# Query tiles of the routing stage start on rows that are not yet normed; root and shift are applied to their products

## The reference

```
def rms_norm(x, g, eps=RMS_EPS):
    y = x32 * lax.rsqrt(jnp.mean(x32 * x32, axis=-1, keepdims=True) + eps)
    return (y * g.astype(jnp.float32)).astype(x.dtype)
...
        mod = (jax.nn.silu(c) @ w_ada[l] + b_ada[l])[:, None, :]
        sh1, sc1, gt1, sh2, sc2, gt2 = jnp.split(mod, 6, axis=-1)
...
        h = h + gt1 * (mixed @ w_out[l])
        xn2 = rms_norm(h, norm2_g[l]) * (1.0 + sc2) + sh2
        h = h + gt2 * peer_ffn(xn2, peer_wq[l], peer_subkeys[l], peer_u[l], peer_v[l])
...
def peer_ffn(xn, wq, subkeys, u_tab, v_tab):
    q = (xt @ wq).reshape(T, PEER_HEADS, 2, PEER_HALF)
    s = jnp.einsum('thpd,hpnd->thpn', q, subkeys).astype(jnp.float32)
    top_s, top_i = lax.top_k(s, PEER_TOPK)
```

## Time and profile before

| | before |
|---|---|
| median of 3 runs | 1678.75 us (1678.7 to 1679.78) |
| profiled execution, its own time | 1680.06 us |
| its span | 1678.1 us |
| PE busy | 1636.5 us, 98% of the span |
| DVE busy | 1238.0 us, 74% |
| ACT busy | 821.5 us, 49% |
| mean granted TensorE clock | 0.998 of full speed |

### The profile page before, as it was taken

One profiled execution on the slowest core, in us unless ns is written; L12 is line 12 of the kernel. 1 busy time (PEld: TensorE's weight loads), 2 busy tenths in 40 slices (PEclk: granted clock), 3 DMA queues, 4 the chain that ended last, 5 costly groups with the idle time before them and its releaser, 6 DMA issues.

```text
span 1678.1 us, 32665 instructions
## 1 busy us (share of the span) xinstructions
PE 1636.5 (98%) x11608; PEld 1440.7 (86%) x11608; DVE 1238.0 (74%) x2593; ACT 821.5 (49%) x1491; POOL 165.5 (10%) x135
## 2 busy tenths in 40 slices
PE   6999999999999999999999999999999999999998
PEld 4887988899988888888888888888899777999998
DVE  6885537748989988788888888888446565578887
ACT  3544111345469944555555555555444246554443
POOL 0020000007700000000000000000037214100000
PEclk9999999999999999999999999999999999999999
DMA  8742135765742288777777777777454651245553
GB/s 345 289 145 89 40 126 209 269 202 172 220 151 63 89 261 261 233 238 237 237 236 234 237 233 238 237 236 233 142 175 132 221 183 39 90 137 186 178 186 126
DMA packets 102623, 316.94 MB, mean 189 GB/s; under 512 B 11393, under 2 KB 21377, under 8 KB 102145
## 3 DMA queue, kind: packets, MB, share of 16 engines
q1 hardware_dynamic: 101664, 311.27, 57.4%
q10 hardware_dynamic: 864, 4.39, 0.7%
HBM read 309.71 MB, written 5.90 MB: 188 GB/s over the span
## 4 chain that ended last, share of the span: by engine, by line
PE 68%; DVE 11%; ACT 9%; issue 8%; DMA 2%; DVEq 0%; POOL 0%; SPq 0%; ACTq 0%
PE bank L490 9%; PE bank L492 9%; PE bank L491 9%; PE bank L505 4%; PE bank L1949 4%; PE bank L1951 4%; PE bank L1953 4%; PE bank L1212 3%; ACT whi L479 3%; PE bank L506 2%; ACT arena L1912 2%; PE bank L465 2%; PE bank L1498 2%; ACT arena L1903 2%; DVE xn L2071 2%
## 5 line engine op out<-in xcount | busy, mean ns | idle before, releaser
L484 DVE TENSOR_TENSOR wlo<-wring,whi 128x1024 fp32r<-128x1024 f32 x340 | 414.2, 1223 | 88.9 <-ACT whi L479 80.0
L479 ACT CAST whi<-wring 128x1024 fp32r<-128x1024 f32 x386 | 403.7, 1046 | 115.7 <-PE bank L1953 49.5
L490 PE MATMUL bank<-xboth,whi 128*128 128x256 f32 x1184 | 340.3, 287 | 5.7 <-DVE wlo L484 2.6
L491 PE MATMUL bank<-xboth,whi 128*128 128x256 f32 x1184 | 334.9, 283 | 0.0
L492 PE MATMUL bank<-xboth,wlo 128*128 128x256 f32 x1184 | 334.9, 283 | 0.0
L490 PEld LDWEIGHTS bank<-xboth,whi 128*128 128x128 f32 x1184 | 226.9, 192 | 11.1 <-issue 5.6
L491 PEld LDWEIGHTS bank<-xboth,whi 128*128 128x128 f32 x1184 | 227.1, 192 | 0.7 <-issue 0.5
L492 PEld LDWEIGHTS bank<-xboth,wlo 128*128 128x128 f32 x1184 | 227.0, 192 | 0.0
L505 PE MATMUL bank<-xboth,whi 128*128 128x512 f32 x616 | 220.8, 397 | 0.0
L484 POOL TENSOR_TENSOR wlo<-wring,whi 128x1024 fp32r<-128x1024 f32 x46 | 117.6, 2561 | 855.2 <-ACT whi L479 855.0
L506 PE MATMUL bank<-xboth,wlo 128*128 128x256 f32 x616 | 172.7, 280 | 0.0
(11 more groups left out here) (384 smaller groups left out, 2730.2 us busy)
## 6 DMA issues: line engine op xcount, KB each, us to landing
wring<-in_w SPq DMA_DIRECT2D x463, 512.0 KB, 4.1
arena<-in_ada SPq DMA_DIRECT2D x48, 512.0 KB, 7.2
xn<-in_ada SPq DMA_DIRECT2D x96, 256.0 KB, 3.2
h_spill<-arena SPq DMA_DIRECT2D x37, 128.0 KB, 2.0
arena<-h_spill SPq DMA_DIRECT2D x37, 128.0 KB, 4.2
wring<-in_w SPq DMA_DIRECT2D x6, 384.0 KB, 4.8
wring<-in_w SPq DMA_DIRECT2D x8, 256.0 KB, 3.3
arena<-in_const ACTq DMA_DIRECT2D x1, 1215.0 KB, 5.5
```

Source lines behind the costliest of these rows:

```text
L479: act.copy(whi[:, n % HSLOTS, :], wring[:, n % SLOTS, :]).then_inc(hi_ready, 1)
L484: eng.tensor_tensor(wlo[:, n % SLOTS, :], wring[:, n % SLOTS, :], whi[:, n % HSLOTS, :].bitcast(F32), ALU.subtract).then_inc(lo_ready, 1)
L490: pe.matmul(out, h, xh, start=start, stop=False, **kw)
L491: pe.matmul(out, h, xl, start=False, stop=False, **kw)
```

## The change

The first nine of the sixteen query tiles (`RAW1` = 9) are computed on `raw`, a split copy of `hT` times the gain, without the root. Two more columns in each block of `raw` hold the shift, so that a matmul has 258 columns and column 256 of the bank holds the product of weights and shift. DVE multiplies the bank by the reciprocal root into `qp` and copies that column out (`raw_scale`), and ACT adds it (L1811 of the changed kernel). The normed rows, which the other seven tiles and later stages need, are made between these steps, block by block. The rows of `ada` for the scale are fetched first, so that the gain is known before w_out starts. The last two sums of squares move from w_out into the first pair of tiles, and the 22 matmuls on the identity are gone.

```
+        def raw_upper(act, n, m):
+            act.activation(raw[:, m, 0, 0:S], hT[:, m, :], ACT.Identity, scale=gsc[:, n, m:m + 1]).then_inc(x_hi, 1)
+        def raw_rest(dve, n, m):
+            dve.wait_ge(x_hi, XHI[n] + m + 1)
+            dve.scalar_tensor_tensor(raw[:, m, 1, 0:S], hT[:, m, :], gsc[:, n, m:m + 1], raw[:, m, 0, 0:S].bitcast(F32),
+                                     ALU.mult, ALU.subtract).then_inc(x_lo, 1)
+        def raw_pair(pe, norm, n, outs):
+            for k0, k1 in ((0, KT - 2), (KT - 2, KT)):
+                for i in range(2):
+                    pe.wait_ge(lo_ready, nth_split[n + i])
+                    for k in range(k0, k1):
+                        pe.wait_ge(x_lo, XLO[norm] + k + 1)
+                        mm = raw_three(pe, outs[i], n + i, k)
+                    if k1 == KT:
+                        mm.then_inc(tile_done, 1)
+                    elif i == 0:
+                        for m in range(k1, KT):
+                            norm_sum(pe, norm, m, nsq[norm])
+        def raw_scale(dve, out, bk, rt, add):
+            dve.tensor_tensor(out, bk[:, 0:S], rt, ALU.mult)
+            return dve.tensor_copy(add, bk[:, S:S + 1])
+        def norm_gain(dve, n, k, rt):
+            dve.scalar_tensor_tensor(xn[:, k, :], hT[:, k, :], gsc[:, n, k:k + 1], rt, ALU.mult,
+                                     ALU.mult).then_inc(x_scaled, 1)
+        def norm_upper(act, n, k, shift):
+            act.wait_ge(x_scaled, KT * n + k + 1)
+            act.activation(xhi[:, k, :], xn[:, k, :], ACT.Identity, bias=modc(shift, k)).then_inc(x_hi, 1)
+        def norm_rest(dve, n, k, shift):
+            dve.wait_ge(x_hi, XHI[n] + KT + k + 1)
+            dve.scalar_tensor_tensor(xlo[:, k, :], xn[:, k, :], modc(shift, k), xhi[:, k, :].bitcast(F32), ALU.add,
+                                     ALU.subtract).then_inc(x_lo, 1)
...
         def pe_w_out(pe):
...
-            for m in (KT - 2, KT - 1):
-                norm_sum(pe, 1, m, nsq[1])
-            pe_warm(pe, 7, 22)
...
         def act_w_out(act):
...
+                raw_upper(act, 1, m)
                 act_square(act, 1, m, nsq[1])
...
         def pe_route(pe):
...
+            raw_pair(pe, 1, w, (bank[r % BANKS], bank[(r + 1) % BANKS]))
+            for t in range(2, RAW1):
+                pe.wait_ge(lo_ready, nth_split[w + t])
+                pe.wait_ge(ring_free, r + t - BANKS + 1)
+                raw8(pe, bank[(r + t) % BANKS], w + t).then_inc(tile_done, 1)
+            pe.wait_ge(x_lo, XLO[2])
+            ring_tiles_split(pe, "wq", RAW1)
...
             for t in range(COUNT["wq"]):
                 act_hi_of(act, "wq", t + 2)
                 tile_wait(act, "wq", t)
-                act.copy(qp[:, t, :], ring_bank("wq", t)[:, 0:S]).then_inc(ring_free, 1)
+                if t < RAW1:
+                    act.wait_ge(raw_scaled, t + 1)
+                    act.activation(qp[:, t, :], qp[:, t, :], ACT.Identity, bias=raw_add1[:, t:t + 1]).then_inc(ring_free, 1)
+                    for k in (2 * t - 4, 2 * t - 3):
+                        if 0 <= k < KT:
+                            norm_upper(act, 1, k, 3)
...
             norm_root(dve, v, 1, rtn[1])
-            norm_scale(dve, rtn[1])
-            x_rest(dve, 1)
-            lo_phase(dve, "wq", 2)
+            lo(2)
+            norm_gain(dve, 1, 0, rtn[1])
+            norm_gain(dve, 1, 1, rtn[1])
+            scale(0)
+            scale(1)
+            lo(3)
+            for t in range(2, RAW1):
+                lo(t + 2)
+                for k in (2 * t - 2, 2 * t - 1):
+                    if k < KT:
+                        norm_gain(dve, 1, k, rtn[1])
+                    else:
+                        norm_rest(dve, 1, k - KT, 3)
+                scale(t)
+            for t in range(RAW1 + 2, COUNT["wq"]):
+                lo(t)
```

More of the change, by code:

```diff
@@ L167 @@
 ARENA = 41920
+RAW = S + 2
+RAW_AT = 18736
+RAWNORMS = (1, )
+XHI, XLO = [0], [0]
+for _name in range(4):
+    XHI.append(XHI[-1] + (2 * KT if _name in RAWNORMS else KT))
+    XLO.append(XLO[-1] + (2 * KT if _name in RAWNORMS else KT // 2))
 AFTER_WHI = S * NK + 2 * KT * S + HSLOTS * D
@@ L209, in build_layer_pair @@
         sb("xn_end", [P, AHALF])
-        sb("arena_start", [P, S * NK])
+        sb("arena_start", [P, RAW_AT])
+        raw = sb("raw", [P, KT, 2, RAW], F32R)
+        sb("arena_middle", [P, S * NK - RAW_AT - 2 * KT * RAW])
         xboth = sb("xboth", [P, KT, 2, S], F32R)
@@ L533, in act_square @@
             act.activation(sq[:, m, :], hT[:, m, :], ACT.Square).then_inc(sq_ready, 1)
-            if n in (1, 3) and m == KT - 3:
+            if n in (1, 3) and m == 1:
                 act_table(act, ACT.Sqrt)
@@ L595, in x_rest_pair @@
         def x_rest_pair(eng, n, k):
[L597 removed]
+            eng.wait_ge(x_hi, XHI[n] + k + 2)
             eng.tensor_tensor(xlo[:, k:k + 2, :], xn[:, k:k + 2, :], xboth[:, k:k + 2, 0, :].bitcast(F32),
@@ L609, in split_pair @@
                 if k % 2 == 0:
-                    pe.wait_ge(x_lo, 4 * norm + k // 2 + 1)
+                    pe.wait_ge(x_lo, XLO[norm] + k // 2 + 1)
                 for i in range(2):
@@ L618, in build_layer_pair, with raw_shift_upper, raw_shift_rest @@
         rtn = [arena[:, 5632:5888], arena[:, 28672:28928], r2["rot"][:, 0:256], rF["sg"][:, 0:256]]
+        raw_scaled = sem("raw_scaled")
+        def raw_shift_upper(act, shift):
+            act.copy(raw[:, :, 0, S:RAW], wide(modc(shift, 0, KT), 2))
+        def raw_upper(act, n, m):
+            act.activation(raw[:, m, 0, 0:S], hT[:, m, :], ACT.Identity, scale=gsc[:, n, m:m + 1]).then_inc(x_hi, 1)
+        def raw_shift_rest(dve, n, m, shift):
+            dve.wait_ge(x_hi, XHI[n] + m + 1)
+            dve.tensor_tensor(raw[:, :, 1, S:RAW], wide(modc(shift, 0, KT), 2), raw[:, :, 0, S:RAW].bitcast(F32), ALU.subtract)
@@ new lines, in raw_rest, with raw_three @@
+        def raw_rest(dve, n, m):
+            dve.wait_ge(x_hi, XHI[n] + m + 1)
+            dve.scalar_tensor_tensor(raw[:, m, 1, 0:S], hT[:, m, :], gsc[:, n, m:m + 1], raw[:, m, 0, 0:S].bitcast(F32),
+                                     ALU.mult, ALU.subtract).then_inc(x_lo, 1)
+        def raw_three(pe, out, n, k):
+            return three(pe, out[:, 0:RAW], n, k, raw[:, k, 0, :], raw[:, k, 1, :], k == 0, k == KT - 1)
+        def raw_pair(pe, norm, n, outs):
[10 more added lines that the diff above has]
+                            norm_sum(pe, norm, m, nsq[norm])
@@ new lines, in raw8 @@
+        def raw8(pe, out, n):
+            for k in range(KT):
+                mm = raw_three(pe, out, n, k)
+            return mm
+        def raw_scale(dve, out, bk, rt, add):
[4 more added lines that the diff above has]
+                                     ALU.mult).then_inc(x_scaled, 1)
@@ new lines, in norm_upper, with norm_whole @@
+        def norm_upper(act, n, k, shift):
[5 more added lines that the diff above has]
+                                     ALU.subtract).then_inc(x_lo, 1)
+        def norm_whole(act, n, k, shift):
+            act.wait_ge(x_lo, XLO[n] + KT + k + 1)
+            act.activation(xn[:, k, :], xn[:, k, :], ACT.Identity, bias=modc(shift, k)).then_inc(xn_ready, 1)
@@ L857, in ada @@
                     sp.wait_ge(ada_used, 3 * KT + i - BSLOTS + 1)
-                sp.dma_start(aringb[:, i % BSLOTS, :], a["ada"][3 * KT + i]).then_inc(blanded[i % BSLOTS], 16)
+                sp.dma_start(aringb[:, i % BSLOTS, :], a["ada"][late_row(i)]).then_inc(blanded[i % BSLOTS], 16)
             sp.wait_ge(t_new, 10)
@@ L1638, in dve_proj @@
                 dve_late_ada(dve, m)
+                if m == SCALE_AT:
+                    dve.wait_ge(ada_used, 4 * KT)
+                    dve_add_bias(dve, v, 4 * KT, 5 * KT)
+                    dve_gsc(dve, v, 1)
+        SCALE_AT = next(j for j in range(KT) if dots_before(j + 1) >= KT)
+        SHIFT_AT = next(m for m in range(KT) if dots_before(KT + m + 1) >= 2 * KT)
+        RAW1 = KT + 1
+        raw_add1 = arena[:, 28928:28928 + RAW1]
         def dve_late_ada(dve, j):
@@ L1659, in act_w_out @@
                 act.wait_ge(ring_free, RING0["w_out"] + m + 1)
+                if m == SHIFT_AT + 1:
+                    raw_shift_upper(act, 3)
+                raw_upper(act, 1, m)
                 act_square(act, 1, m, nsq[1])
@@ L1684, in act_subk @@
         def act_subk(act):
-            act.wait_ge(xn_ready, 2 * KT)
+            act.wait_ge(ring_free, RING0["w_out"] + KT)
             act.dma_start(rK["subk"], a["subk"]).then_inc(subk_loaded, 16)
@@ L1712, in act_route @@
                 tile_wait(act, "wq", t)
-                act.copy(qp[:, t, :], ring_bank("wq", t)[:, 0:S]).then_inc(ring_free, 1)
+                if t < RAW1:
[5 more added lines that the diff above has]
+                else:
+                    act.copy(qp[:, t, :], ring_bank("wq", t)[:, 0:S]).then_inc(ring_free, 1)
+                    for k in (2 * (t - RAW1), 2 * (t - RAW1) + 1):
```

(45 more changed lines are left out.)

12 lines of the change are left out of this document (5 added, 7 removed).

## The result

The changed kernel takes 1686.14 us (median of 6, 1685.19 to 1690.04), against 1678.63 us for the kernel before, measured beside it (median of 6). The ratio is 1.0047, with a 95% interval of 1.0037 to 1.0057: slower by 6 to 10 us. The forecast was 1686.

What follows compares the result with a forecast made beforehand. The prediction took PE as the bound, except for a 7.5 us gap after w_out. Idle 13.05 less lead 7.35 gives 5.7 slower, plus 1.7 for a clock dip: 1678.75 + 7.4 = 1686.1, forecast 1686, range 1681 to 1689.5.

Steps and rivals of the forecast that it cites:

- The start of the pair: Between w_out and the first query tile: PE goes on at once at 325.05, so 7.5 us can be won.
- The lead at tile 2: Third query tile: starts at 331.35 instead of 338.7, a lead of 7.35 us.
- The round: Raw query tiles: ACT's cast and DVE's scaling wait on each other, 4.79 us long, 3.97 short; PE needs 2.88.
- The one open term: ACT's addition with one pointer operand, not in the trace: 0.41 us from start to start, bounds 0.31 and 0.49.
- the circle: The closed chain of waits between ACT and DVE in the raw query tiles: 4.79 us, closed by latency, not work.
- The pause before tile 9: Tenth query tile: PE stands 5.9 us, waiting for DVE's rests of blocks 6 and 7, until 364.6.
- The clock: After the pause ahead of tile 9: one dip of PE's clock, 1.7 us of work lost; bounds none and 3.4.
- The sum: Whole kernel: idle 13.05 us less lead 7.35 is 5.7 slower; with the dip's 1.7, 7.4 slower.
- Faster: Rival: ACT's cast runs far enough ahead, the round never holds PE, the 7.35 us lead stays: 1671.4 us; chance 0.06.
- The rival without a dip: The round as forecast, but PE's clock does not fall: 5.7 us slower, 1684.5 us; chance 0.18.
- the one with dearer rounds: Rival: long rounds of 5.1 us, six adding 1.5, and low clock costing 3.4: 1689.4 us; chance 0.12.
- DVE's new instructions in proj and w_out: Two small ones in proj, some 0.5 us, hidden by a wait; one 0.40 us subtraction per w_out tile, fitting by 0.4.

Runs made afterwards that it cites:

- the repeated one: The changed kernel run once more, unaltered, on another occasion: 1687.13 us, ratio 1.0048 to the kernel before.
- the two edits on top: On cast_ahead: DVE's two block instructions put ahead of the lower half, 1670.21 us; with that, the third weight tile made before the root, 1670.54 us.
- scale_first: Changed kernel, but DVE scales tile t ahead of the lower half of weight tile t + 2, not behind it: 1675.49 us, ratio 0.9992 to the kernel before.
- cast_ahead: Changed kernel, but ACT casts weight tile t + 3 ahead of its wait for scaled tile t: 1671.74 us, ratio 0.9959 to the kernel before.

## Why the prediction was right

**The start of the pair** went as forecast: query matmuls behind the last sum in w_out, none of the 7.5 us left. Before, PE began them 332.59 - 325.05 = 7.5 us after the last residual. Now the first one starts at 324.29 in PE's timeline, level with the residual at 324.25.

**The lead at tile 2** was mis-sized, 7.35 forecast and 6.5 measured (tile 2 at 331.35, 7.1 us after the residual instead of 6.3). Two terms make up the 0.8. One is the two sums of squares inside the pair, taken as 0.43 us for both. The chain shows `PE bank L553 x4`, 0.88 us: each sum is two records, 0.43. The earlier trace rows had shown `L544 x2` for one sum. The other is the sum of block 5, which PE still makes between w_out's last matmul and the first query one (`324.21 0.43 PE bank L553 x2`). The working left it out and let PE go on at the residual's start; by the chain PE goes on 0.39 later, at 324.64. From the end of the two sums to tile 2 it is 3.67 us, as worked out (3.65).

**The round** was right in place and size. Forecast for ACT's casts of weight tiles 3 to 10: 333.0, 334.35, 339.15, 343.95, 348.75, 353.5, 357.5, 361.5. In the changed kernel:

```profile
332.99 1.03 ACT L488 CAST whi<-wring 128x1024 fp32r<-128x1024 f32 x1
...
334.34 1.03 ACT L488 CAST whi<-wring 128x1024 fp32r<-128x1024 f32 x1
...
339.13 1.03 ACT L488 CAST whi<-wring 128x1024 fp32r<-128x1024 f32 x1
...
343.92 1.03 ACT L488 CAST whi<-wring 128x1024 fp32r<-128x1024 f32 x1
...
357.49 1.04 ACT L488 CAST whi<-wring 128x1024 fp32r<-128x1024 f32 x1
361.48 1.03 ACT L488 CAST whi<-wring 128x1024 fp32r<-128x1024 f32 x1
```

The distances, 4.79 and 3.99, are the forecast. That the clock readings agree too is partly luck: the execution came to this place 0.8 us earlier than the one of before, a lead that it had from at least 135 us on, and lost the same 0.8 to the sums. The one open term, ACT's form with one pointer operand, was taken half way at 0.41 from start to start; two of them (L688) last 0.90 and one 0.51, so it is 0.40. The hand-over from DVE to ACT was taken as 0.03 and is 0.09 (the column copy ends at 342.61, the addition starts at 342.70); cast to lower half is 1.06 instead of 1.08, the other terms are 0.01 or 0.02 off, and the sum comes out the same, which is in small part luck. Three experiments carry the mechanism: with the circle opened at either joint the raw tiles run at 2.87 us, and with 0.8 us taken out of it the round is 0.8 us shorter.

**The pause before tile 9** was right. Forecast and view count differently: the view's 5.6 begins at the end of tile 8's last matmul, the forecast's 5.9 where the next tile would have started. The first matmuls of tiles 8 and 9 are

```profile
355.84 0.39 PE L499 MATMUL bank<-raw,whi 128*128 128x258 f32 x1 [1.66 <-DVE wlo L493]
364.62 0.58 PE L499 MATMUL bank<-xboth,whi 128*128 128x256 f32 x1 [5.64 <-DVE xboth L693]
```

and 364.62 - 355.84 - 2.88 = 5.90. Counted so, tiles 3 and 5 wait 1.11 and 0.37 and tiles 6 to 8 1.91 each, all in all 13.1 us, against 13.05 forecast. The pause goes when the circle goes (0.4 left), and it is 2.5 where only the order of DVE's last step holds the rest of the last block.

**The clock** dipped as forecast, but for longer. The term was one dip with 1.7 us of work lost, sized by the dip at the kernel's start; this one kept half speed from about 364 to past 370. Tile 9 starts at 364.62 and the last copy at 387.74, 23.12 us, where the run with identity matmuls and a full clock has 20.45: 2.7 us were lost in this execution, and 2.2 in the repeated one. That lies between the forecast's 1.7 and its upper bound of 3.4. At half the clock the matmuls do not take twice as long, though. In the chain a matmul of the dip and one behind it are

```profile
366.48 0.21 PE bank L500
...
371.27 0.12 PE bank L500
```

and 24 matmuls at full clock take 2.88 us, in the dip 5.1. So a us at 0.50 costs some 0.44 us, and the 6.1 us from 364.6 to 370.7 cost 2.7.

**The sum.** In this stage the loss is 9.4 us, not 7.4: 0.8 from the sums of squares and 1.0 from the longer dip, the rest small. The profiled executions differ by 6.3 us only, because the one of before had lost time elsewhere. The same instructions show a lag of -0.8 us before the change's place (w_out's matmuls at 294.2 instead of 295.0), +8.6 at the scores (L1703 at 379.6, now 388.2), +7.8 at the end of the experts and +6.5 after the next norm. The last 1.3 is a dip of the clock behind 1190 us in the execution of before, which the one of after hasn't at its place; what the 0.8 inside the experts' phase is stays open. By the medians the loss is 7.5 us on the first occasion and 8.9 on the second. So the forecast of 7.4 stands within the interval, while its terms were 2 us short in the stage: part of the agreement of 1686 with 1686.14 is chance.

**The rivals.** "Faster" was right about what could be had: 7.35 us with the round open, of which 5.8 were measured in the stretch once the circle was cut, and 6.5 and 6.8 with the two edits on top. The rival without a dip and the one with dearer rounds did not occur; of the second only the longer low clock did; DVE's new instructions in proj and w_out were hidden, the residuals of w_out's last two tiles stay 3.89 us apart.

The rule of the Trainium skill that was weighed against the change ("TensorE: Matmul & The Clock Gate", why this matters for your kernels) held: the trace agrees, with 0.50 after the pause of 5.6 us. In scale_first 0.50 also followed a pause of 2.5 us, which is shorter than the gaps that the page warns of; there the measurement decides.

## What to carry to other kernels

Two engines that both have slack can still be the bound, when each waits for the other once per tile in fixed order. Write down, for each wait, what stands ahead of the instruction that releases it in its own list, and go on until the walk ends at PE or comes back to where it began; if it comes back, the durations along it are the period, whatever the busy shares are. Then move work that only needs the slow engine's last tile (here the cast of the next weight) ahead of the wait for the other engine: it turned some 8 us lost into 6 to 7 us won with the same instructions.

## What the runs showed of the hardware that was not expected

- After a pause of 5.6 us PE's clock was at 0.50 for 6.8 us (363.9 to 370.7, read in stretches of half a us), with PE busy from 364.6 on. After the pauses of 2.5 us at the start and in scale_first it was there for half as long, 3.4 us (24.3 to 27.7 and 357.0 to 360.4). In the first case it fell 0.7 us before PE went on, in scale_first 1.4 us after.
- At 0.50 the split matmuls follow each other in 0.21 us, at 1.00 in 0.12, so the dip costs less than half of its length.
- A dip is not always preceded by a long pause. In the kernel before, the clock was at 0.50 from 1191.7 to 1195.1 with a pause of 0.71 us ahead of 1188.96; the changed kernel has a pause of 0.70 us at that place of its program and no dip. What decides there no run shows.
- A matmul with 258 columns in split precision costs no more than one with 256: in cast_ahead raw tiles of 24 matmuls run at 2.87 us, normed ones at 2.88.
